# Inner norms finished one token tile at a time in a hybrid decoder block on one Trainium2 core

## What is computed

```python
def rms_norm(x, g):
    xf = x.astype(jnp.float32)
    y = xf * lax.rsqrt(jnp.mean(xf * xf, axis=-1, keepdims=True) + NORM_EPS)
    return (y * g.astype(jnp.float32)).astype(x.dtype)
...
        x = x + merged @ w_out[i]
        x = x + conv_glu_ffn(rms_norm(x, g_ffn[i]), w_up[i], conv_w[i], conv_b[i], w_down[i])
        ple_gate = jax.nn.sigmoid(rms_norm(x, g_ple[i]) @ w_ple_gate[i])
        x = x + ple_gate * (p[i] @ w_ple[i])
    return rms_norm(x, g_final)
```

## Time and profile before

| | |
|---|---|
| Time, median of 3 runs | 1136.35 us (1136.14 to 1141.2) |
| Span of the profiled execution | 1143.6 us |
| Profiled execution's own time | not recorded beside its span |
| TensorE busy | 1081.0 us, 95% |
| VectorE, ScalarE, GpSimd busy | 439.6, 445.4, 360.6 us |
| Mean granted TensorE clock | 0.975 of full speed |

### The profile page before, as it was taken

How to read it: one execution, slowest core, us unless ns; L and a number is a source line. 1 busy time by engine, 2 the same in 40 slices (tenths; PEclk the granted TensorE clock), 3 DMA queues, 4 the chain that set the end, 5 groups by cost and what they waited for, 6 DMA issues and landing times.

```text
span 1143.6 us, 13614 instructions
## 1 busy us (share of the span) xinstructions
PE 1081.0 (95%) x5575; PEld 904.1 (79%) x5575; DVE 439.6 (38%) x712; ACT 445.4 (39%) x718; POOL 360.6 (32%) x163
## 2 busy tenths in 40 slices
PE   3999999998899999999999979999999999999894
PEld 3885887866698999999888868888888888888783
DVE  4110286567643534343266154434334430000413
ACT  4244445244533242423353354444444432321533
POOL 1442443302021011010244424444444444444331
PEclk9999999969899999999999989999999999999998
DMA  8232433300001001010124313333333333222311
GB/s 242 74 94 54 100 85 86 96 3 19 1 1 32 25 19 38 20 38 19 55 89 170 92 56 93 101 102 92 92 103 99 93 111 105 97 92 92 111 56 74
DMA packets 114339, 86.45 MB, mean 76 GB/s; under 512 B 2740, under 2 KB 99782, under 8 KB 114278
## 3 DMA queue, kind: packets, MB, share of 16 engines
q1 hardware_dynamic: 113638, 83.51, 24.6%
q10 hardware_dynamic: 640, 2.06, 0.5%
HBM read 83.47 MB, written 2.10 MB: 75 GB/s over the span
## 4 chain that ended last, share of the span: by engine, by line
PE 75%; ACT 2%; DVE 2%; issue 1%; POOL 0%; ACTq 0%
PE bank L447 11%; PE bank L449 11%; PE bank L448 11%; PE bank L590 9%; PE bank L479 7%; PE bank L481 7%; PE bank L480 7%; PE bank L558 3%; PE bank L580 3%; PE bank L607 2%; PE bank L598 1%; PE bank L573 1%; PE bank L671 1%; PE bank L670 1%; PE bank L682 1%
## 5 line engine op out<-in xcount | busy, mean ns | idle before, releaser
L427 POOL TENSOR_TENSOR w_lo<-raw,w_hi 128x1024 fp32r<-128x1024 f32 x145 | 349.6, 2411 | 673.7 <-ACT w_hi L761 673.7
L761 ACT ACTIVATE w_hi<-raw 128x1024 fp32r<-128x1024 f32 x145 | 153.7, 1060 | 419.6 <-issue 203.5
L447 PE MATMUL bank<-hT_hi,w_hi 128*128 128x512 f32 x728 | 291.6, 401 | 0.0
L449 PE MATMUL bank<-hT_hi,w_lo 128*128 128x512 f32 x728 | 284.5, 391 | 0.0
L448 PE MATMUL bank<-hT_lo,w_hi 128*128 128x512 f32 x728 | 284.1, 390 | 0.0
L449 PEld LDWEIGHTS bank<-hT_hi,w_lo 128*128 128x128 f32 x728 | 137.1, 188 | 29.1
L447 PEld LDWEIGHTS bank<-hT_hi,w_hi 128*128 128x128 f32 x728 | 137.3, 189 | 27.0 <-ACT Aa L832 0.8
L448 PEld LDWEIGHTS bank<-hT_lo,w_hi 128*128 128x128 f32 x728 | 137.4, 189 | 26.7 <-issue 0.7
L1405 DVE SCALAR_TENSOR_TENSOR cbuf<-bank,params,cbuf 128x511 f32<-128x511 f32 x48 | 36.0, 750 | 138.0 <-ACT cbuf L1016 138.0
L479 PE MATMUL bank<-w_hi,g_hi 128*128 128x512 f32 x192 | 74.8, 389 | 0.0
L481 PE MATMUL bank<-w_hi,g_lo 128*128 128x512 f32 x192 | 74.7, 389 | 0.0
(11 more groups left out here) (254 smaller groups left out, 1522.5 us busy)
## 6 DMA issues: line engine op xcount, KB each, us to landing
raw<-in_w_up_dram SPq DMA_DIRECT2D x48, 512.0 KB, 3.9
raw<-in_w_in_dram SPq DMA_DIRECT2D x33, 512.0 KB, 3.9
raw<-in_w_down_dram SPq DMA_DIRECT2D x24, 512.0 KB, 3.6
raw<-in_w_gate_dram SPq DMA_DIRECT2D x16, 512.0 KB, 3.9
raw<-in_w_out_dram SPq DMA_DIRECT2D x8, 512.0 KB, 3.6
raw<-in_w_ple_gate_dram SPq DMA_DIRECT2D x8, 512.0 KB, 3.7
xs<-in_x_dram SPq DMA_DIRECT2D x4, 512.0 KB, 9.4
raw<-in_w_branch_a_dram SPq DMA_DIRECT2D x4, 512.0 KB, 3.5
```

The source lines that it names most:

```text
L427: nc.gpsimd.tensor_tensor(w_lo[:, n % W_SLOTS, :], raw[:, n % RAW_SLOTS, :], w_hi[:, n % W_SLOTS, :].bitcast(F32), ALU.subtract).then_inc( ...
L447: nc.tensor.matmul(o, wh, ah, start=first, stop=False)
L449: return nc.tensor.matmul(o, wl, ah, start=False, stop=last)
L761: nc.scalar.activation(w_hi[:, u % W_SLOTS, :], raw[:, u % RAW_SLOTS, :], ACT.Copy) \
```

## The change

At both inner norms each token tile is finished by itself once its second half is added. VectorE's list becomes: add 0, add 1, [sum, reciprocal, scaling of tile 0], add 2, [those of tile 1], add 3, [tile 2], [tile 3]. ScalarE takes the root of a tile behind its square, and ahead of the first square of half 1 stands a root of a constant, into a column of `stat` that nothing reads, so that the table is loaded there. TensorE first takes all eight banks and then transposes by token tile, eight at a time, each tile as soon as it is scaled; a bank is complete with its fourth tile.

```diff
+            def transposed_by_token(tag, src, name):
+
+                os = [begin(tag, k) for k in range(KD)]
+                for m in range(NT):
+                    pe.wait_ge(*done("dve", name, m))
+                    for k in range(KD):
+                        mm = nc.tensor.transpose(os[k][:, m * P:(m + 1) * P], src[:, m, k * P:(k + 1) * P], ident)
+                        if m == NT - 1:
+                            mm.then_inc(*step("pe", (tag, k)))
...
-            for m in range(NT):
-                pe.wait_ge(*done("dve", "xn_b", m))
-            transposed("nb", xn_b, KD)
+            transposed_by_token("nb", xn_b, "xn_b")
...
-            for m in range(NT):
-                pe.wait_ge(*done("dve", "xn_c", m))
-            transposed("nc", xn_c, KD)
+            transposed_by_token("nc", xn_c, "xn_c")
...
                     if m == NT - 1:
                         before(("out", h, 3))
+                    if h == 1 and m == 0:
+                        nc.scalar.activation(stat[:, epsc + 2:epsc + 3], stat[:, epsc:epsc + 1], ACT.Sqrt).then_inc(*step("act"))
                     act.wait_ge(*previous("act"))
                     squares_of("nb", xr, cbuf[:, 0, :, :], m, h)
-            root("nb")
+                    if h:
+                        root("nb", m, m + 1)
...
-            def rms_scaled(tag, dst, name):
-                mean_square(tag)
-                dve.wait_ge(*done("act", "rms", tag, 0))
-                V.reciprocal(stat[:, rstd:rstd + NT], stat[:, rms:rms + NT]).then_inc(*step("dve"))
-                dve.wait_ge(*previous("dve"))
+            def rms_scaled(tag, dst, name, m):
+                mean_square(tag, m, m + 1)
+                dve.wait_ge(*done("act", "rms", tag, m))
+                V.reciprocal(stat[:, rstd + m:rstd + m + 1], stat[:, rms + m:rms + m + 1]).then_inc(*step("dve"))
+                dve.wait_ge(*previous("dve"))
+                V.tensor_scalar(dst[:, m, :], xr[:, m, :], stat[:, rstd + m:rstd + m + 1], None, ALU.mult) \
+                    .then_inc(*step("dve", (name, m)))
+
+            def last_half(sums, tag, dst, name):
+
                 for m in range(NT):
-                    V.tensor_scalar(dst[:, m, :], xr[:, m, :], stat[:, rstd + m:rstd + m + 1], None, ALU.mult) \
-                        .then_inc(*step("dve", (name, m)))
+                    residual(sums, 1, m, ("x_" + tag, 1, m))
+                    if m:
+                        rms_scaled(tag, dst, name, m - 1)
+                rms_scaled(tag, dst, name, NT - 1)
```

More of the change, by code:

```diff
@@ L1027, in _ @@
                         before(("down", h, NF // 2 - 1))
+                    if h == 1 and m == 0:
+                        nc.scalar.activation(stat[:, epsc + 2:epsc + 3], stat[:, epsc:epsc + 1], ACT.Sqrt).then_inc(*step("act"))
                     act.wait_ge(*previous("act"))
                     squares_of("nc", xr, cbuf[:, 1, 2:4, :], m, h)
+                    if h:
+                        root("nc", m, m + 1)
                 if h == 0:
                     gained_hi("np", None, 2, pT_hi)
-            root("nc")
             for h in range(2):
@@ L1375, in residual @@
                 V.tensor_tensor(x, psum((tag, h, m))[:, :], x, ALU.add).then_inc(*frees("dve", (tag, h, m), *marks))
-            def rms_scaled(tag, dst, name):
-                mean_square(tag)
-                dve.wait_ge(*done("act", "rms", tag, 0))
-                V.reciprocal(stat[:, rstd:rstd + NT], stat[:, rms:rms + NT]).then_inc(*step("dve"))
+            def rms_scaled(tag, dst, name, m):
+                mean_square(tag, m, m + 1)
+                dve.wait_ge(*done("act", "rms", tag, m))
+                V.reciprocal(stat[:, rstd + m:rstd + m + 1], stat[:, rms + m:rms + m + 1]).then_inc(*step("dve"))
                 dve.wait_ge(*previous("dve"))
+                V.tensor_scalar(dst[:, m, :], xr[:, m, :], stat[:, rstd + m:rstd + m + 1], None, ALU.mult) \
+                    .then_inc(*step("dve", (name, m)))
+            def last_half(sums, tag, dst, name):
                 for m in range(NT):
-                    V.tensor_scalar(dst[:, m, :], xr[:, m, :], stat[:, rstd + m:rstd + m + 1], None, ALU.mult) \
-                        .then_inc(*step("dve", (name, m)))
+                    residual(sums, 1, m, ("x_" + tag, 1, m))
+                    if m:
+                        rms_scaled(tag, dst, name, m - 1)
+                rms_scaled(tag, dst, name, NT - 1)
             dve.wait_ge(xr_in, 16)
[L1387 to L1390, removed]
+            for m in range(NT):
+                residual("op", 0, m, ("x_nb", 0, m))
+            last_half("op", "nb", xn_b, "xn_b")
             gained_lo("nb", "g_ffn", KD, hT_hi, hT_lo, "hT_lo")
@@ L1414, in _ @@
             g_rest(NF - 1)
[L1415 to L1420, removed]
+            for m in range(NT):
+                residual("dn", 0, m, ("x_nc", 0, m))
+            gained_lo("np", None, 2, pT_hi, pT_lo, "pT_lo")
+            last_half("dn", "nc", xn_c, "xn_c")
             gained_lo("nc", "g_ple", KD, hT_hi, hT_lo, "hT_lo")
```

## The result

| | before | changed |
|---|---|---|
| Median of all runs beside each other | 1141.34 us (16 runs, 1136.14 to 1146.02) | 1146.99 us (16 runs, 1139.68 to 1152.0) |
| Ratio of the times | 1 | 1.0046, between 1.0026 and 1.0066 |
| Profiled execution: span, mean granted clock | 1143.6 us, 0.975 | 1142.1 us, 0.980 |
| Profiled execution's own time | not shown | 1143.97 us |

The changed kernel is slower by 5.2 us of 1141.3 (0.0046 x 1141.3; 3.0 to 7.5 by the interval). The forecast was a difference of +4.5 us. Its absolute time, 1140.9 us, was 6 us too low, and the median lies above the range. In every execution here the time is the span and 1.8 to 2.0 us more.

The account below looks back on a forecast made before the run. It took TensorE's matmuls as the bound, with work in 1081.0 of the span's 1143.6 us. nb -1.8 and nc +6.35 sum to +4.5, put on the median 1136.35: 1140.9 us, range 1136.9 to 1143.4.

Parts of the forecast that it names:

- nb: Norm before the feed-forward part: earlier matmuls gain 2.2 us, the clock takes back 0.4; -1.8 us, between -2.2 and -0.7.
- table load ahead: At both norms, the load moves into ScalarE's pause ahead of the first square; cost nothing, gain nothing.
- the copy behind root 2: ScalarE's weight split at nb, queued behind the third root, comes 2.8 us later than before.
- the last sum ending with GpSimd: At nb VectorE's last sum still waits until GpSimd's weight work ends, at 665.7 us.
- nc: Last inner norm, ahead of `w_ple_gate`: a loss of +6.35 us, between +3.4 and +7.3.
- `w_ple` late: At nc the second `w_ple` unit waits for its weight from GpSimd and starts 1.35 us late.
- wait for `pple`: At nc TensorE waits about 3.3 us for the last copy of `w_ple` sums before its transposes.
- Sum +4.5: nb's -1.8 and nc's +6.35 added: +4.5 us, between +1.2 and +6.6.
- Rival 1: At both norms the clock stays low; nb keeps 0.7, nc loses 7.3: +6.6, 1142.9 us; chance 0.25.
- Rivals 2 and 3: nc: copies on time or bank wait hidden, 1134.5 us, chance 0.08; both norms: change works as worded, 1130.5 us, chance 0.05.
- rival 3: GpSimd no longer holds the last sum: -3.9 at nb, -2 at nc, 1130.5 us; chance 0.05.
- Slower 0.27, same 0.68: Whole kernel: chance 0.27 of slower by over 0.5% (5.7 us), 0.68 of the same, 0.05 of faster.

Follow-up runs that it names:

- e1: The changed kernel's edits at nb alone, with nc as in the kernel before; ratio 0.9988 against the kernel before.
- e6: The kernel before with only the root of a constant ahead of each second half's first square, loading the table there; ratio 1.0013.
- e2: The changed kernel's edits at nc alone, with nb as in the kernel before; ratio 1.0049 against the kernel before.
- e5: The kernel before with only the transposes by token tile at nc, all eight banks taken first; ratio 1.0050.
- e4: The kernel before with roots, sums and scalings by token tile at nc, transposes by bank as before; ratio 1.0024.
- e10: The kernel before with roots, sums and scalings by token tile at nb, transposes by bank as before; ratio 1.0014.
- e0: The kernel before run once more with nothing changed; ratio 1.0003, twelve runs from 1136.49 to 1145.63 us.
- e3: e1 with the last weight copy at nb put behind the fourth root; ratio 0.9962 against the kernel before.
- e8: The edits of e3 and e7 together; median 1132.45 us, ratio 0.9919 against the kernel before.
- e7: The kernel before with the later weight copy of the `w_ple` part moved behind the `hT_hi` work; ratio 0.9973.
- e9: e8 with a `w_ple_gate` weight copy moved earlier, behind the final norm's second square; median 1127.95 us, ratio 0.9883 against the kernel before.

## Why the prediction came out as it did

- **"I take the difference from the trace and put it on the median: 1140.9 us."** This is the step that failed. The median of the three runs shown, 1136.35, is the fast end of the program's own spread: beside the changed kernel its median was 1141.34, in other sets 1140.12 to 1141.82. The warning was in the text: a span of 1143.6, 7.3 us above that median, was passed over although it was a fourth execution of the same program, whose time would be 1145.4 by the later runs. +4.5 on 1141.34 gives 1145.8, 0.1% under what was measured; the range allowed 0.5 us of scatter, while the executions of one program lie 10 us apart. (By the working given, its lower end would be 1137.1, not 1136.9; nothing hangs on that.)
- **nb, "-1.8, between -2.2 and -0.7".** Measured -2.5 in the pair of profiles, -3.3 in e1. The chain was right: table load ahead worth nothing (e6), the copy behind root 2, the last sum ending with GpSimd. The size was outside the range: two terms were too large, since I laid durations end to end, and instructions overlap by 0.1 us or so: the copy came 2.3 us later and not 2.8, and the last scaling 0.3 us later and not 0.9. That brings the first `w_up` matmul 3.2 us forward, not 2.5.
- **nc, "+6.35, between +3.4 and +7.3".** Measured +6.5. Its terms: `w_ple` late by 0.8 us (forecast 1.35, from the same overlap), wait for `pple` 3.34 (3.3), so the transposes start 0.5 us earlier than forecast; transposes 6.51 us long (forecast 1.3 more than 3.96, measured 2.55 more, as all but the last few ran slow and not 14); first `w_ple_gate` matmul at B + 28.55 (forecast 28.07); from there to the end of the stage 0.4 us less than before, where the forecast took nothing. An error of +1.0 us, between the start of the transposes and that matmul, against two of -0.5 and -0.4: that the term fits to 0.1 us is luck. In e2 and e5 the transposes took 5.35 us, what I had forecast; both happen.
- **Sum +4.5.** Stages +4.0, runs +5.2 (3.0 to 7.5). That the sum fits so well is in part luck, as the terms show; that nb gains and nc loses more is shown. Since e2 + e1 give the whole within their intervals, the edits don't need to act on each other. The 1.9 us of the stretch behind nc are in this pair of profiles a fall of the clock behind the 2.2 us pause for `w_lo` in `w_ple_gate`. In the changed kernel (windows, as above):

```profile
1116.00:1118.00 2.00, 2.00 (x6) 1.62 (x7) 0.00 (x0) 0.00 (x0) 2.00 (x1) 0.67 0.00 0
1118.00:1120.00 2.00, 2.00 (x6) 1.51 (x6) 0.00 (x0) 0.00 (x0) 0.26 (x1) 0.50 0.00 0
1120.00:1122.00 2.00, 2.00 (x10) 1.65 (x9) 0.00 (x0) 0.00 (x0) 0.00 (x0) 0.98 0.00 0
```

In before that pause ends at 1119.10, and the clock stays at 1.00 behind it (timeline, then window):

```profile
1119.10 0.50 PE L479 MATMUL bank<-w_hi,hT_hi 128*128 128x512 f32 x1 [2.23 <-POOL w_lo L427]
...
1118.00:1120.00 2.00, 0.90 (x4) 0.77 (x5) 0.00 (x0) 0.01 (x1) 2.00 (x2) 1.00 0.00 0
```
The fall stood in the profiled executions of the changed kernel, e1, e2, e4 and e10, and not in those of before, e0, e3 and e5 to e8. One execution of each doesn't tell whether the change makes it likelier; that stays open.
- **Rival 1, the clock stays low through both gaps.** At nb this rival was wrong: the first `w_up` matmuls were slow (0.77 us), but the clock was back at 1.00 by 663, and the stage got shorter by more than forecast. At nc it was right for the transposes, nearly all of which ran slow. That transposes alone can't bring the clock back is not borne out: before, it rose at 670.4 with nothing but transposes since 666.43, and in the changed kernel it rose between 1074 and 1076 with nothing but transposes since 1069.91. The Trainium skill's rule (TensorE: Matmul & The Clock Gate, section "Part 4: PE-mode transpose") says otherwise; here the measurement decides.
- **Rivals 2 and 3.** "The copies at nc are not late, or the bank wait is hidden" is refuted by the wait of 3.34 us, "the change works as its words say" by the 1.66 us of the last sum. e3 makes at nb what rival 3 spoke of, and is 4.3 us faster than the kernel before (0.0038 x 1141.8).
- **"Slower 0.27, same 0.68".** The ratio, 1.0046, lies just inside the 0.5%, with its interval on both sides of it.

## What to carry to other kernels

When a step is split to start sooner, list what its new first instruction waits for: here 32 transposes that had waited bank by bank came to wait for the last reader of eight banks (e5, +0.5%). Look which weight copy stands in front of the chain on the engine that does both, and what another engine's bulk work holds for its duration; moving two such copies (e8) gave, with nb's edits, 9.2 us, where the change as it stands costs 5.2. Put a difference onto the level of many runs, and treat a profiled span far from the shown median as one more run.

## What was not expected of the hardware

- One program on one core, nothing changed, spreads from 1136.0 to 1146.4 us, and the time goes with the granted clock: about 1 us for each 0.001 of its mean. After pauses of 2 to 3 us the clock fell in some executions and not in others: after the `pple` wait in all three kernels that had it, behind the pause for `w_lo` in `w_ple_gate`, 2.2 to 2.3 us in all of them, in five profiled executions of twelve.
- With all but the last few at 1.2 GHz 32 transposes take 6.51 us, at 2.4 GHz 3.96 or less (3.65 in e7); with a part at either, 5.35 (e2, e5).
- A VectorE sum of 128x1 elements takes 0.15 us alone and 1.66 us beside GpSimd's subtraction, and one of 128x512 takes 0.69 us alone and 2.83 us beside it (e9); both have both their inputs in SBUF. VectorE's adds from a PSUM bank took 0.69 us beside GpSimd's work too (at 655.23 in before, with GpSimd at work from 655.06).
